# Layer 0's later modulation tiles get buffers of their own, and one gate-and-x load is issued earlier

## The reference, cut to what matters

```python
shift, scale, gate = split(silu(cond) @ w_mod + b_mod, 3)   # w_mod: 2048 x 6144 per layer
h = rmsnorm(x, norm_g) * (1 + scale) + shift
q, k, v, z_a, xbc, z_s, dt_f, dt_b, g_a, g_s = split(h @ w_in)  # 2048 x 19584
... conv, bidirectional SSD scan -> y_s;  attention -> o_a
merged = sigmoid(g_a) * ((o_a * silu(z_a)) @ w_pa) + sigmoid(g_s) * (y_s @ w_ps)
x = x + gate * (merged @ w_out)
```

## Time and profile before

| | us |
|---|---|
| median of 3 runs | 2888.45 (2887.72 to 2888.83) |
| the profiled execution | 2879.7 |
| its span | 2877.8 |
| PE busy in the span | 2793.3 (97%) |
| DVE busy | 1925.2 (67%) |
| ACT busy | 1483.4 (52%) |

### The profile page before, as it was taken

One profiled execution on the slowest core, in us unless ns is written; L12 is line 12 of the kernel. 1 busy time (PEld: TensorE's weight loads), 2 busy tenths in 40 slices (PEclk: granted clock), 3 DMA queues, 4 the chain that ended last, 5 costly groups with the idle time before them and its releaser, 6 DMA issues.

```text
span 2877.8 us, 40977 instructions
## 1 busy us (share of the span) xinstructions
PE 2793.3 (97%) x16512; PEld 2370.0 (82%) x16512; DVE 1925.2 (67%) x2398; ACT 1483.4 (52%) x2210; POOL 203.9 (7%) x259
## 2 busy tenths in 40 slices
PE   7999999999999999999889999999999999999997
PEld 4888998888766898877669988988888888897886
DVE  2487899887666445566655888898876654554555
ACT  3356776774333445533334557767753434544443
POOL 0001111120000000000100011211110000000000
PEclk9999999999999999999999999999999999999999
DMA  9945455546777654567786545455466664554665
GB/s 395 336 158 165 165 169 171 179 156 209 281 275 274 199 167 146 170 240 274 273 321 206 174 158 172 162 169 180 160 202 241 247 210 166 161 177 153 206 220 174
DMA packets 166589, 594.21 MB, mean 206 GB/s; under 512 B 20244, under 2 KB 22548, under 8 KB 166016
## 3 DMA queue, kind: packets, MB, share of 16 engines
q1 hardware_dynamic: 155376, 558.24, 56.1%
q0 software_dynamic: 10960, 33.34, 4.0%
q10 hardware_dynamic: 64, 0.02, 0.0%
HBM read 577.85 MB, written 13.66 MB: 206 GB/s over the span
## 4 chain that ended last, share of the span: by engine, by line
PE 74%; DVE 11%; DMA 9%; ACT 2%; issue 2%; SPq 1%; DVEq 0%; POOLq 0%; POOL 0%; ACTq 0%
PE PM L432 15%; PE PM L444 15%; PE PM L433 14%; PE PM L437 7%; PE PM L448 7%; PE PM L438 7%; PE A L699 5%; DVE w_l L410 3%; DVE arena L498 3%; DVE arena L1441 2%; DMA raw<-in_w_out 2%; DMA raw<-in_w_in 2%; DMA raw<-in_w_ps 2%; ACT w_h L405 2%; DMA Zt<-in_w_mod 2%
## 5 line engine op out<-in xcount | busy, mean ns | idle before, releaser
L410 DVE TENSOR_TENSOR w_l<-raw,w_h 128x1024 fp32r<-128x1024 f32 (+1 forms) x880 | 1056.4, 1213 | 818.9 <-ACT w_h L405 812.0
L405 ACT ACTIVATE w_h<-raw 128x1024 fp32r<-128x1024 f32 (+1 forms) x880 | 903.3, 1046 | 824.9 <-PE PM L444 337.1
L432 PE MATMUL PM<-w_h,hT_h 128*128 128x512 f32 x1408 | 563.5, 400 | 6.2 <-ACT w_h L405 4.4
L433 PE MATMUL PM<-w_h,hT_l 128*128 128x512 f32 x1408 | 549.6, 390 | 0.0
L437 PE MATMUL PM<-hT_h,w_h 128*128 128x256 f32 x1920 | 486.4, 291 | 5.5 <-ACT w_h L405 2.5
L438 PE MATMUL PM<-hT_l,w_h 128*128 128x256 f32 x1920 | 469.7, 282 | 0.0
L432 PE MATMUL PM<-w_h,Z 128*128 128x512 f32 x1024 | 407.8, 398 | 24.1 <-ACT w_h L405 20.3
L433 PE MATMUL PM<-w_h,Z 128*128 128x512 f32 x1024 | 400.6, 391 | 0.0
L437 PEld LDWEIGHTS PM<-hT_h,w_h 128*128 128x128 f32 x1920 | 366.5, 191 | 20.5 <-issue 11.9
L444 PE MATMUL PM<-w_l,hT_h 128*128 128x512 f32 x1408 | 377.7, 390 | 1.7 <-DVE w_l L410 1.7
L438 PEld LDWEIGHTS PM<-hT_l,w_h 128*128 128x128 f32 x1920 | 367.1, 191 | 6.2 <-issue 4.8
(11 more groups left out here) (200 smaller groups left out, 2335.1 us busy)
## 6 DMA issues: line engine op xcount, KB each, us to landing
raw<-in_w_in SPq DMA_DIRECT2D x608, 512.0 KB, 4.1
raw<-in_w_ps SPq DMA_DIRECT2D x128, 512.0 KB, 4.6
raw<-in_w_mod SPq DMA_DIRECT2D x112, 512.0 KB, 3.8
Zt<-in_w_mod SPq DMA_DIRECT2D x80, 512.0 KB, 14.1
raw<-in_w_pa SPq DMA_DIRECT2D x64, 512.0 KB, 4.4
raw<-in_w_out SPq DMA_DIRECT2D x64, 512.0 KB, 6.0
arena<-in_states POOLq DMA_DIRECT2D x16, 512.0 KB, 3.7
out_state_f_out<-arena POOLq DMA_DIRECT2D x16, 256.0 KB, 2.8
```

The lines of the kernel that those rows point to most:

```text
L405: act.activation(w_h[:, k % RING, :, 0:n], half_raw(k, n), ACT.Copy).then_inc(hi_ready, 1)
L410: dve.tensor_tensor(w_l[:, k % RING, :, 0:n], half_raw(k, n), w_h[:, k % RING, :, 0:n].bitcast(F32), ALU.subtract).then_inc(lo_ready, 1)
L432: pe.matmul(tok_out(s), hi[:, kt, tk], wh, start=kt == 0, stop=False, skip_group_check=True)
L433: pe.matmul(tok_out(s), lo[:, kt, tk], wh, start=False, stop=False, skip_group_check=True)
```

## The change

The 96 tiles of groups 4 to 9 leave the ring `raw`. Only the 16 tiles of group 11, in layer 1, stay in it. Groups 4 to 8 go to five homes of 1024 columns in `arena`, at one set of offsets in PS and at another in PA. Group 9 goes to the eight slots of `Zt` that held `aT`, before the fillers. Each tile is now issued behind the load of the half two further on. SP waits, where a home is used again, for the tile five before it (eight before it in `Zt`). It also waits for the place to be free at the first tile of groups 4 and 7, and at the first eight of group 9. The tile is used behind the same half as before. Group 9's spots change from every 1.5 halves, from OUT's half 0 on, to every 1.33 halves, from half 3 on. The split between PE and DVE is the same. DVE's partial sums of groups 5 and 7 move, to columns of `x2` and to `Zt`. `gate_and_x(0)` is issued right behind the end of attention, in both layers.

```diff
+PS_HOMES = (3072, 4096, 5120, 6144, 7168)
+PA_HOMES = (2048, 4096, 5376, 6400, 7424)
+HOMES = 5
...
+def later_tiles():
+    spots = [8 * (PH_PS + 3) + 7 * i // 5 for i in range(PS_TILES)]
+    spots += [8 * (PH_PA + 2) + 3 * i // 2 for i in range(PA_TILES)]
+    spots += [8 * PH_OUT + 3 + 4 * i // 3 for i in range(KT)]
+    after = {at: GROUP_TILES + i for i, at in enumerate(spots)}
...
+def home(m):
+    i = m - GROUP_TILES
+    return i % HOMES, (PS_HOMES if i < PS_TILES else PA_HOMES)[i % HOMES], i // HOMES
+
+HOME_LOAD = {at + 2: m for at, m in RAW_TILES.items() if not in_raw(m)}
...
-        if half in RAW_TILES:
+        if half in RAW_TILES and in_raw(RAW_TILES[half]):
             of_tile[RAW_TILES[half]] = n
...
+        def tile_done(eng, m):
+            if on_dve(m):
+                eng.wait_ge(mod_added, DVE_TILES.index(m) + 1)
+            else:
+                eng.wait_ge(mod_used, PE_TILES.index(m) + 1)
...
-                if FILLERS <= m < FILLERS + 8:
+                if Q9 <= m < Q9 + 8:
                     chunk_done(sp, PH_PA + 7)
-                if m >= FILLERS + 8:
-                    sp.wait_ge(mod_used, PE_TILES.index(m - 8) + 1)
+                if m >= Q9 + 8:
+                    tile_done(sp, m - 8)
                 sp.dma_start(Zt[:, z_slot(m), :], mod_words(m)).then_inc(z_loaded[z_slot(m)], DMA)
+            def tile_home(m):
+                slot, at, turn = home(m)
+                if turn:
+                    tile_done(sp, m - HOMES)
+                if m == GROUP_TILES:
+                    sp.wait_ge(s_("yT_read"), NG)
+                    sp.wait_ge(s_("st_out"), NG * DMA)
+                    sp.wait_ge(s_("st_out_b"), NG * DMA)
+                if m == GROUP_TILES + PS_TILES:
+                    sp.wait_ge(s_("aT_ready"), 4)
+                    sp.wait_ge(s_("v_out"), DMA)
+                sp.dma_start(arena[:, at:at + MOD_N], mod_words(m)).then_inc(tile_at_home[slot], DMA)
             def half(L, c, i, w, block):
                 load(w[L, block, i])
                 k = K(c, i)
-                if k in RAW_TILES:
+                if k in RAW_TILES and in_raw(RAW_TILES[k]):
                     load(mod_words(RAW_TILES[k]))
+                if k in HOME_LOAD:
+                    if in_z(HOME_LOAD[k]):
+                        tile_to_z(HOME_LOAD[k])
+                    else:
+                        tile_home(HOME_LOAD[k])
...
                 wait_alone(pool, s_("aT_ready"), L * 4 + 4 + ONE)
                 end_phase(pool)
+                gate_and_x(0)
                 after_phase(pool, L, 8)
...
-                gate_and_x(0)
                 gate_and_x(1)
```

More of the change, by code:

```diff
@@ L86, in K, with z_turn, in_raw @@
     return 8 * L * CHUNKS + (i // 2 * 2 * FIRST + 2 * lc + i % 2 if lc < FIRST else 8 * lc + i)
+PS_TILES = 3 * KT
+PA_TILES = 2 * KT
+Q9 = GROUP_TILES + PS_TILES + PA_TILES
+PS_HOMES = (3072, 4096, 5120, 6144, 7168)
+PA_HOMES = (2048, 4096, 5376, 6400, 7424)
+HOMES = 5
 def in_z(m):
-    return m < GROUP_TILES or FILLERS <= m < FILLERS + KT
+    return m < GROUP_TILES or Q9 <= m < FILLERS + KT
 def z_slot(m):
[L96 to L110, removed]
-    return after
-RAW_TILES = raw_tiles()
+    return m % Z_SLOTS if m < GROUP_TILES else (m - Q9) % (Z_SLOTS // 2)
+def z_turn(m):
+    return m // Z_SLOTS if m < GROUP_TILES else GROUP_TILES // Z_SLOTS + (m - Q9) // (Z_SLOTS // 2)
+def later_tiles():
[3 more added lines that the diff above has]
+    after = {at: GROUP_TILES + i for i, at in enumerate(spots)}
+    spots = [8 * CHUNKS + 8 * (PH_PS + 3) + 4 * i for i in range(KT)]
+    after.update((at, FILLERS + KT + i) for i, at in enumerate(spots))
+    return after
+RAW_TILES = later_tiles()
+def in_raw(m):
+    return m >= FILLERS + KT
+def home(m):
+    i = m - GROUP_TILES
+    return i % HOMES, (PS_HOMES if i < PS_TILES else PA_HOMES)[i % HOMES], i // HOMES
+HOME_LOAD = {at + 2: m for at, m in RAW_TILES.items() if not in_raw(m)}
 def on_dve(m):
     q, kt = divmod(m, KT)
-    return q == 11 or (kt % 3 != 2 and kt < 15 if q < 7 else kt % 2 == 0)
+    return q == 11 or 3 < q < 7 and kt % 3 != 2 and kt < 15 or 6 < q < 10 and kt % 2 == 0
 DVE_TILES = [m for m in RAW_TILES.values() if on_dve(m)]
@@ L350, in build @@
         raw_loaded = [sem(f"raw_loaded{i}") for i in range(SLOTS)]
+        tile_at_home = [sem(f"tile_at_home{i}") for i in range(HOMES)]
         z_loaded = [sem(f"z_loaded{i}") for i in range(Z_SLOTS)]
@@ L385, in slot_free, with tile_loaded @@
                     sp.wait_ge(lo_ready, i + 1)
-                elif on_dve(i):
-                    sp.wait_ge(mod_added, DVE_TILES.index(i) + 1)
-                else:
-                    sp.wait_ge(mod_used, PE_TILES.index(i) + 1)
+                else:
+                    tile_done(sp, i)
+        def tile_loaded(eng, m):
+            if in_z(m):
+                eng.wait_ge(z_loaded[z_slot(m)], (z_turn(m) + 1) * DMA)
+                return Zt[:, z_slot(m), :]
+            if in_raw(m):
+                n = LOAD_OF_TILE[m]
+                eng.wait_ge(raw_loaded[n % SLOTS], (n // SLOTS + 1) * DMA)
+                return raw[:, n % SLOTS, :]
+            slot, at, turn = home(m)
+            eng.wait_ge(tile_at_home[slot], (turn + 1) * DMA)
+            return arena[:, at:at + MOD_N]
         def half_loaded(eng, k):
@@ L460, in mod_tile @@
                     pe.wait_ge(s_("modsb_read"), q)
[L461 to L468, removed]
+            held = tile_loaded(pe, m)
             for j in range(4):
@@ L476, in mod_sums @@
             if q in (4, 5, 6, 11):
[L477 to L480, removed]
+                return x2[:, s, 1024:2048] if q == 5 else arena[:, 1024 + s * MOD_N:1024 + (s + 1) * MOD_N]
+            if q in (7, 8):
+                return Zt[:, q + 3 + 4 * s, :]
             return arena[:, 5376 + s * MOD_N:5376 + (s + 1) * MOD_N]
@@ L485, in tile_add @@
             q, kt = divmod(m, KT)
-            n, at = LOAD_OF_TILE[m], DVE_TILES.index(m)
+            at = DVE_TILES.index(m)
             first = at == 0 or DVE_TILES[at - 1] // KT != q
-            dve.wait_ge(raw_loaded[n % SLOTS], (n // SLOTS + 1) * DMA)
-            if first and q in (6, 9):
-                dve.wait_ge(s_("mod_summed"), q - 5)
+            held = tile_loaded(dve, m)
+            if first and q == 6:
+                dve.wait_ge(s_("mod_summed"), 1)
+            if first and q == 9:
+                tile_done(dve, max(k for k in PE_TILES if k < Q9))
             if not first:
@@ L495, in tile_add @@
                 if first:
-                    ins = dve.tensor_scalar(acc, raw[:, n % SLOTS, :], c, None, ALU.mult)
+                    ins = dve.tensor_scalar(acc, held, c, None, ALU.mult)
                 else:
-                    ins = dve.scalar_tensor_tensor(out=acc, in0=raw[:, n % SLOTS, :], scalar=c, in1=acc, op0=ALU.mult, op1=ALU.add)
+                    ins = dve.scalar_tensor_tensor(out=acc, in0=held, scalar=c, in1=acc, op0=ALU.mult, op1=ALU.add)
             ins.then_inc(mod_added, 1)
@@ L2042, in layer @@
                 end_phase(pool)
[L2043 to L2047, removed]
                 def gate_and_x(j):
@@ L2054, in gate_and_x @@
                         pool.dma_start(xch[par][:, s], x_in[:, cs]).then_inc(s_(f"gb_loaded{par}"), DMA)
+                wait_alone(pool, s_("aT_ready"), L * 4 + 4 + ONE)
+                end_phase(pool)
+                gate_and_x(0)
+                after_phase(pool, L, 8)
+                if not more:
+                    pool.dma_start(fng, a["final_norm_g"].unsqueeze(0).to_broadcast([P, D_MODEL])).then_inc(s_("fng_loaded"), DMA)
                 def x_store(j):
```

## The result

| | before | changed |
|---|---|---|
| median, us | 2888.64 (2887.72 to 2889.68, 4 runs) | 2841.73 (2839.59 to 2843.53, 4 runs) |
| ratio | | 0.9842, 95% interval 0.983 to 0.9853 |
| profiled execution, us | 2879.7 | 2842.2 |
| its span, us | 2877.8 | 2839.8 |

The changed kernel is 46.9 us faster by the medians, and 38.0 us by the spans of the two profiles. The forecast was 36.0 us less, 2852 in a range from 2843 to 2868. The direction and the cause were right. The miss of 10.7 us splits in two. The profiled execution came to 2842.2 where 2843.7 was forecast, 1.5 of it.

What follows compares the result with a forecast made beforehand. PE, busy 97% of the span, bounds the kernel, so only its standstill can go. 39.7 us of standstill less 3.7 residue gave 36.0 us off 2888.45, so 2852, in a range from 2843 to 2868.

Steps and rivals of the forecast that it cites:

- Standstill of 15.7, 5.7 and 18.3 us: Layer 0's PS, PA and OUT: PE's time lost beyond its extra instructions, 39.7 us together, the most to come back.
- The ring is the cause: Layer 0's PS: tiles leave the five-slot ring 2.9 halves, 8.5 us of PE's work, against a turn of 9.4.
- SP's waits for adds: Layer 0's PS: SP waits 116.3 us for DVE's adds before it may load again, a sign for the ring.
- ACT's waits for loads: Layer 0's PS: ACT waits 142.1 us for raw loads, against 3.5 in layer 1's PS, a sign for the ring.
- The turn after the change: Ring without tiles: the same turn of 9.4 us against 14.6 of PE's work, 5 us to spare.
- The residue, 3.7 us: Standstill taken to remain in layer 0: 2 us in OUT, 1 in PS, 0.7 in PA.
- the rival in which transfers bound OUT: Layer 0's OUT stays at its mean 307 GB/s, 112 us; gain 23 us, time 2866; chance 0.20.
- I carry the difference over unchanged: Whole kernel: the median stays 8.75 us above the profiled execution, as before the change.
- more comes back: The 8.75 us of median over profile may be stalls of the same ring: up to 45 us go, 2843; chance 0.08.
- Waits on SP cost nothing: SP's waits for homes to be free: 0 taken, at worst 0.6 us for each of 34 PE tiles, 20 us.
- The gate load is hidden: gate_and_x(0), four loads of 256 KB, leaves OUT for PA's first 16 halves, some 160 us earlier.
- The slower rival: Landings grow to 14.1 us and DVE waits in order: 129 us more standstill, 2978; turning point 11.1; chance 0.03.

Runs made afterwards that it cites:

- q9_in_ring: The changed kernel with group 9's tiles (layer 0's OUT) kept in the raw ring, behind the same halves: 2855.44 us.
- ring3: The changed kernel with a raw ring of three slots instead of five: 2933.77 us.
- issue_at_0: The changed kernel with each tile issued behind the load of its own half (at) instead of at+2: 2842.04 us.
- late_gate: The changed kernel with gate_and_x(0) back behind the end of phase PA: 2842.34 us.
- issue_at_5: The changed kernel with each tile issued behind the load of half at+5 instead of at+2: 2975.11 us.
- the last version: The changed kernel with 15 of 16 tiles of groups 4-6, 13 of 7-8 and 12 of 9 on DVE, 13 on PE: 2819.56 us.

## Why the prediction was wrong by its range, and right in its mechanism

- **Standstill of 15.7, 5.7 and 18.3 us.** Right to a tenth: 15.7, 5.8 and 18.2 came back. The method was to count the extra instructions of a stage, price each by the distance of starts, and take the rest as standstill. It gave what PE's idle column showed only in part (30.3 us).
- **The ring is the cause.** Shown by q9_in_ring, stage by stage, and by the kernel before with four slots (2974.90 us). ring3 agrees in PS. Whether a larger ring would have served as well as homes is open. SP's waits for adds fit. ACT's waits for loads were a weaker sign than I took them for, as ring3 shows. The turn after the change was put too long: by the slots that PS can do with, it is nearer 6.9 us than 9.4, because the add had left it.
- **The residue, 3.7 us.** A failed term, the smaller one. The three stages kept nothing of it, but the stretch behind OUT, which the sum does not have, lost 2.2 us, with a lower clock in it. The net loss is 1.7 us in the span against the 3.7 forecast, and as the profiled execution lies 2.4 us above its span and not 1.9, its forecast was off by 1.5. I gave 2 us of it to OUT, because its last chunk had moved 10.7 MB at 398 GB/s. Those bytes were partly loads made up late: the last half of `w_out` was issued at 1483.24, 17 us before the end of OUT, and in the changed kernel at 1435.62, 24.5 us before it and ahead of the whole last chunk. That chunk moves 288 GB/s in 23.50 us. OUT as a whole ran at 339 GB/s without a wait, so the rival in which transfers bound OUT fell, as its 307 GB/s had been the pace of the ring. The Trainium skill's figure of about 358 GB/s ("DMA: Bandwidth & Descriptors", Specifications), which its row works out as one of two cores' halves of 716, did not hold this one core either: the changed kernel's start carries 407 GB/s over 80 us again. OUT asks for less than 358, so it does not test the figure.
- **"I carry the difference over unchanged".** The step that failed, 9.2 of the 10.7 us. The 8.75 us between the profiled execution of before and its median were not a fixed cost that both kernels pay. Run again, the kernel before has its profiled execution 1.2 us above its median (2887.19 and 2886.02), and the changed kernel 0.5 above (2842.2 and 2841.73). So the first profile was a short execution, not a typical one. Of the 7.5 us by which the second profile's span is longer, 4.8, about two thirds, lie in the stages where the ring runs short. The rival "more comes back", with a chance of 0.08 and 2843, is what happened. The 2.9 us outside the three stages are not explained.
- **Waits on SP cost nothing.** Right, and with more room than I gave: issue_at_0 holds SP far longer for nothing.
- **The gate load is hidden.** Right for the changed kernel (late_gate), though in the kernel before the same edit is worth 6.3 us.
- **The slower rival.** Its condition did not come about (homes landed in 5.7 us, 11.1 was the turning point), but the part of it in which DVE waits in order for a tile is real, as issue_at_5 shows.

## What to carry to other kernels

Look at what a prefetch ring holds besides what it is there for. A guest that is released later, here a tile that waits for an add, takes a slot and makes the turn longer too, and moving the guests out gave back all that PE had lost in these stages. Whether more slots would do the same was not tried. A wait ahead of the bounding engine is not yet a loss: look at the distance between that engine's own starts. Two edits that ease the same shortage don't add up: measure each against both ends. When the stage to be mended is one that stands still, a single profile may show too little of it, so weigh its distance from the median as part of what may come back.

## What the runs showed of the hardware that was not expected

- The DMA engines carried 339 GB/s over OUT's 96.76 us, and 348 over 94.15 us in the last version, at busy shares of 0.91 and 0.94, and PE's list of waits in the changed kernel's OUT holds 0.5 us, none of it for a load.
- PE's lower clock level came with a wait and outlasted it. In the kernel before, run again, PE waited 4.61 us for a weight (below). The matmuls behind it start 0.43 us apart until 1434, and 0.23 apart after that. The granted share was 0.77 over 1425 to 1440, a mix of the levels 2.4 and 1.2 GHz. In the changed kernel's OUT it is 1.00.

```profile
1428.84 0.80 PE L432 MATMUL PM<-w_h,Z 128*128 128x512 f32 x1 [4.61 <-ACT w_h L405]
...
1429.86 0.63 PE L432 MATMUL PM<-w_h,Z 128*128 128x512 f32 x1
1430.29 0.63 PE L433 MATMUL PM<-w_h,Z 128*128 128x512 f32 x1
...
1435.19 0.40 PE L432 MATMUL PM<-w_h,Z 128*128 128x512 f32 x1
1435.42 0.39 PE L433 MATMUL PM<-w_h,Z 128*128 128x512 f32 x1
```
